# Output sums of a state-space layer moved behind head steps, keys in places of their own, the last state rows returned in two halves

## The chip, the cores and the metric

One Trainium2 chip, one of its cores. Times are microseconds of device time for one execution of the whole program. The engines are TensorE (PE; its weight loads are PEld), VectorE (DVE), ScalarE (ACT), GpSimd (POOL) and SyncE (SP), which here issues all the transfers.

## The reference: what is computed

One inference step of a two-layer decoder, 512 prompt tokens and 8 sample tokens (520 columns in all) of width 1024. Layer 0 mixes by a diagonal state-space model (S5: 48 groups of 16 channels, 64 states each) and by attention to 256 memory tokens; layer 1 attends to shared keys and values. The change lies in layer 0's mixing:

```python
y = (einsum('btgp,gcp->btgc', hr, c_re) - einsum('btgp,gcp->btgc', hi, c_im))
y = y.reshape(bsz, t, SEQ_WIDTH) + d_skip * u
y = gelu(y)
y = y * sigmoid(y @ w_glu + b_glu)            # w_glu is 768 x 768: six panels of 128 columns
...
s = einsum('bthd,bmhd->bhtm', q, mk) * ATTN_SCALE   # memory attention of the 8 sample rows
p = softmax(s)
```

All 16 results (both outputs, states, keys, values, convolution tails) are returned.

## The kernel before, in words

The state-space part runs in three thirds (`THIRDS`), t = 0, 1, 2, of 16 groups each. For a third, TensorE turns the input matrices (`bT` jobs, in `bp`), multiplies them with the inputs (`V` jobs), VectorE turns that by powers of the poles, scans it and writes the chunk states `hp`; TensorE makes the short kernels (`K` jobs), ScalarE copies them to `kern`, SyncE spreads `kern` by eight transfers into the block matrix `toep`. The output sums (`Y` jobs, `y_sums(t)`) need `hp` and `toep` of their third. ScalarE copies the sums to `yb`, SyncE writes them to a scratch area in DRAM (`y_store`, nine transfers that reorder rows) and reads them back in the layout of the residual (`y_return`, into `yz`); GpSimd adds them to the skip term (`add_z`), ScalarE applies the Gelu, and VectorE and ScalarE split the result into a high and a low part, `x_hi` and `x_lo`, for the gate's product. The gate's product (`glu`) is six panels, each 6 k-steps of 6 matmuls. Jobs of TensorE that go to the four `misc` banks take them in the order that `misc_jobs` lists; a job waits until the bank of the job four before it has been read.

Between these stand steps of the prompt's memory attention on TensorE (`head_step`, three steps in each of the last two thirds), and the memory attention of the 8 sample rows: a query product per row (`mem_query`), a product and a sum on VectorE (`mem_sample`), which needs the row's keys `mk`, then a softmax over all rows that goes back and forth: `decode_turn` (PE), `decode_spread` (DVE), `decode_max` (PE), `decode_shift` (DVE), `decode_exp` (ACT), `decode_sum` (DVE), `decode_total` (PE), `decode_scale` (DVE), then `mem_sums` (PE).

Every engine executes its own program strictly in the written order, and engines meet by semaphores only. In the order before, `y_sums(t - 1)` stands inside third t, between its `V` and its `K` jobs; `y_sums(2)` stands behind all head steps with two query products ahead of each half. Keys have six places, so that those of rows 6 and 7 are loaded behind the last state rows' return. VectorE does all eight `mem_sample` and the maximum before its first `x_lo`. In the lines of the profile L583 is the helper `load` on SyncE, L2706 the helper that turns a tile, L1206 VectorE's product helper, L2821 and L2826 the two kinds of matmul of `y_sums`, L2866 `mem_query`, L2555 `product`.

ScalarE's `hi(kb, q + 2)` rounds the weights for the panel after next; it reuses the place of panel q, and so waits for panel q to be done:

```python
if it is not None or q >= 2:
    act.wait_ge(panel_done, q - 1)
A.activation(w_hi[slot][:, 0:kb, :], raw[slot][:, 0:kb, :], ACT.Copy).then_inc(hi_made, 1)
```

## Time and profile before

| what | value |
|---|---|
| time before, median of 3 runs | 1567.71 us (1561.73 to 1569.77) |
| the profiled execution: its time | 1564.98 us |
| its span | 1562.6 us |
| busy, PE / PEld / DVE / ACT / POOL | 1425.3 / 1322.5 / 990.8 / 625.1 / 669.7 us |
| mean granted clock of TensorE | 0.957 of full speed (2.4 GHz) |

The span is what the trace covers; the profiled execution took 2.4 us more than its span. TensorE is busy for 91% of the span, but that share is a mean: the stretch of the change, from 160 to 282 us, is one where it stands still for a good part. The rows of the trace for that stretch are shown in a section below. In those, the time in brackets is how long the engine stood idle before the row, and what ended the idle time.

### The profile page before, as it was taken

How to read it: one execution, taken by the hardware profiler on the slowest of the kernel's cores; microseconds unless marked ns; L12 is line 12 of the kernel's file. 1: busy time of each engine (PE TensorE's matmuls, PEld its weight loads, DVE VectorE, ACT ScalarE, POOL GpSimd, SP SyncE). 2: the span in 40 equal slices, each digit the busy share in tenths (PEclk: the TensorE clock that was granted, in tenths of full speed). 3: DMA queues.
4: the chain of work that ended last, by engine and by line, in shares of the span. 5: the costliest groups of instructions: out<-in, count | busy, mean ns of one | idle time of the engine just before them, and what ended most of it. 6: DMA issues, size and time to landing. Idle time of an engine off the chain costs nothing.

```text
span 1562.6 us, 32532 instructions
## 1 busy us (share of the span) xinstructions
PE 1425.3 (91%) x12097; PEld 1322.5 (85%) x12097; DVE 990.8 (63%) x1649; ACT 625.1 (40%) x1058; POOL 669.7 (43%) x428
## 2 busy tenths in 40 slices
PE   6986858888998999999899989998989999999997
PEld 6975637878998999999798976556979999999997
DVE  5769945577776037775847688762677771367755
ACT  4554533345554123332415325541356651243323
POOL 0686332323433344443277888501314444344440
PEclk9996968989999999999999999999989999999999
DMA  5444372222333323232234859995212333233321
GB/s 171 125 98 77 63 195 73 76 62 56 88 90 91 89 81 93 82 101 80 60 114 129 237 157 291 331 349 158 81 50 81 94 102 86 81 94 89 107 80 60
DMA packets 288921, 180.46 MB, mean 115 GB/s; under 512 B 54088, under 2 KB 274412, under 8 KB 288764
## 3 DMA queue, kind: packets, MB, share of 16 engines
q1 hardware_dynamic: 288828, 179.20, 39.6%
q8 instruction: 61, 1.00, 0.3%
q14 instruction: 32, 0.26, 0.1%
HBM read 167.10 MB, written 10.63 MB: 114 GB/s over the span
## 4 chain that ended last, share of the span: by engine, by line
PE 62%; issue 13%; DVE 11%; POOL 5%; ACT 3%; SPq 2%; DMA 2%; DVEq 1%; ACTq 0%; POOLq 0%
PE big L2555 49%; PE big L2621 3%; PE misc L2706 2%; SPq L583 2%; ACT yc L2412 1%; DVE y L1667 1%; POOL s5s L926 1%; PE big L2904 1%; POOL e_tmp L926 1%; POOL e_r L926 1%; DVE tmp L1206 1%; POOL e_i L926 1%; PE misc L3103 1%; DVE rstd L1164 1%; PE big L2652 1%
## 5 line engine op out<-in xcount | busy, mean ns | idle before, releaser
L922 POOL TENSOR_TENSOR w_lo<-raw,w_hi 128x1024 fp32r<-128x1024 f32 (+2 forms) x162 | 425.2, 2626 | 722.8 <-ACT w_hi L2069 722.6
L2555 PE MATMUL big<-x_hi,w_hi 128*128 128x264 f32 x2008 | 415.0, 289 | 17.2 <-POOL w_lo L922 12.4
L2069 ACT ACTIVATE w_hi<-raw 128x1024 fp32r<-128x1024 f32 (+2 forms) x179 | 198.4, 1109 | 526.5 <-PE big L2555 490.6
L2555 PE MATMUL big<-x_hi,w_lo 128*128 128x264 f32 x2008 | 407.7, 285 | 0.0
L2555 PE MATMUL big<-x_lo,w_hi 128*128 128x264 f32 x2008 | 406.0, 284 | 0.0
L2555 PEld LDWEIGHTS big<-x_hi,w_hi 128*128 128x128 f32 x2008 | 312.2, 191 | 23.3 <-issue 16.3
L2555 PEld LDWEIGHTS big<-x_lo,w_hi 128*128 128x128 f32 x2008 | 311.7, 190 | 0.0
L2555 PEld LDWEIGHTS big<-x_hi,w_lo 128*128 128x128 f32 x2008 | 311.1, 190 | 0.0
L1756 DVE SCALAR_TENSOR_TENSOR yc<-uc,convw,yc 128x512 f32<-128x512 f32 x88 | 120.2, 1366 | 113.3 <-ACT yc L2412 113.3
L2555 PE MATMUL big<-h_hi,w_hi 128*128 128x264 f32 x616 | 126.1, 286 | 10.6 <-DVE h_lo L1771 9.1
L2555 PE MATMUL big<-h_lo,w_hi 128*128 128x264 f32 x616 | 124.8, 284 | 0.0
L2555 PE MATMUL big<-h_hi,w_lo 128*128 128x264 f32 x616 | 124.6, 284 | 0.0
L2555 PEld LDWEIGHTS big<-h_hi,w_hi 128*128 128x128 f32 x616 | 95.0, 190 | 11.8 <-DVE h_lo L1771 10.0
L2555 PEld LDWEIGHTS big<-h_lo,w_hi 128*128 128x128 f32 x616 | 95.3, 190 | 0.0
L2555 PEld LDWEIGHTS big<-h_hi,w_lo 128*128 128x128 f32 x616 | 95.3, 190 | 0.0
L1761 DVE SCALAR_TENSOR_TENSOR yc<-uc,convw,yc 128x512 f32<-128x512 f32 x88 | 84.7, 962 | 12.7 <-DVE yc L1759 0.2
L1784 DVE COPY y<-big 128x264 f32 (+1 forms) x32 | 12.2, 423 | 104.7 <-PE big L2555 104.7
L1059 POOL TENSOR_TENSOR areas<-areas,qb 128x768 f32<-128x768 f32 x41 | 74.6, 1833 | 8.7 <-DMA areas<-in_cache_k 7.9
L2412 ACT ACTIVATE yc<-uc,convw 128x520 f32<-128x520 f32 x88 | 72.3, 821 | 0.8
L1146 DVE TENSOR_TENSOR sumsq<-sumsq,sq 128x520 f32<-128x520 f32 x20 | 53.1, 2657 | 11.7 <-ACT sq L2368 9.9
L2408 ACT ACTIVATE newconv<-uc 128x10 f32 (+1 forms) x88 | 18.0, 205 | 103.9 <-DVE uc L1752 103.8
L2652 PE MATMUL big<-x_hi,w_hi 128*128 128x264 f32 (+1 forms) x96 | 38.2, 398 | 17.1 <-DVE x_lo L1196 16.5
(425 smaller groups left out, 2375.1 us busy)
## 6 DMA issues: line engine op xcount, KB each, us to landing
raw<-in_w_up SPq DMA_DIRECT2D x88, 512.0 KB, 3.9
raw<-in_w_down SPq DMA_DIRECT2D x32, 704.0 KB, 4.7
areas<-in_cache_v SPq DMA_DIRECT2D x42, 384.0 KB, 4.6
areas<-in_cache_k SPq DMA_DIRECT2D x41, 384.0 KB, 4.4
raw<-in_w_in SPq DMA_DIRECT2D x16, 512.0 KB, 4.2
raw<-in_w_out SPq DMA_DIRECT2D x16, 512.0 KB, 4.2
raw<-in_w_kv SPq DMA_DIRECT2D x12, 512.0 KB, 4.3
spare<-in_cache_k SPq DMA_DIRECT2D x12, 384.0 KB, 4.4
```

Of the source, the lines that this page charges most:

```text
L583: sp.dma_start(dst, src, **kw).then_inc(s_(sm), 16)
L922: pool.tensor_tensor(w_lo[slot][:, 0:kb, :], raw[slot][:, 0:kb, :], w_hi[slot][:, 0:kb, :].bitcast(F32), ALU.subtract).then_inc(lo_made, 1)
L926: own.do(pool.tensor_tensor(o, a_, b_, op))
L1059: own.tell(pool.tensor_tensor(p, p, qb[b % 2][:].rearrange("p (a d) -> p a d", a=2), ALU.mult), s_("k_product"), n + 1)
L1146: ins = V.tensor_tensor(sumsq[:], sumsq[:], sq[:, m % 2, :], ALU.add)
L1756: st(V.scalar_tensor_tensor(yy[:, 0:T], uu[:, 1:1 + T], w_[1], yy[:, 0:T], ALU.mult, ALU.add))
L1761: st(V.scalar_tensor_tensor(yy[:, 0:T], uu[:, 0:T], w_[0], yy[:, 0:T], ALU.mult, ALU.add))
L2069: A.activation(w_hi[slot][:, 0:kb, :], raw[slot][:, 0:kb, :], ACT.Copy).then_inc(hi_made, 1)
L2412: A.activation(yy[:], uu[:, 2:2 + NT], ACT.Identity, bias=convw[:, 1 - l, bass.ds(it + (f * KH + half * KF + 132), 1)], scale=convw[:, 1 - ...
L2555: ins = pe.matmul(big[2 * slot + b_][:, 0:c1 - c0], w[slot][:, k, :], r[:, c0:c1], start=(k == 0 and n_ == 0), stop=(k == kb - 1 and n_ == 2))
L2621: return pe.matmul(big[2 * slot + b_][:, 0:c1 - c0], w[slot][:, k, :], r[:, c0:c1], start=(k == 0 and n_ == 0), stop=(k == kb - 1 and n_ = ...
L2652: ins = pe.matmul(big[2 * slot + b_][:, 0:c1 - c0], w[slot][:, k, :], r[:, k, c0:c1], start=(k == 0 and n_ == 0), stop=(k == KD - 1 and n_ ...
```

## The change

Five edits, all in layer 0's state-space and gate part.

1. `y_sums(1)` moves from inside third 2 to the end of third 1, behind the head steps 3, 4 and 5. `y_sums(0)` stays. SyncE's `u_load(2)`, the states' return of thirds 0 and 1 and ScalarE's `read_y(1)` move with it.
2. The keys of the 8 sample rows have eight places of their own. Five are loaded inside third 2, ahead of `toep`'s last loading, one behind it, two behind the first gate weights.
3. The last third's output rows are stored in two halves of 8 groups, from a buffer of their own (`yb_last`), and returned in two tiles of 128 rows (`yz_last`); `add_z_tile`, the Gelu and the split follow tile by tile.
4. VectorE makes the `x_lo` of tiles 0 to 3 before `mem_sample` 4 and 5, then tiles 4 and 5, then `mem_sample` 6 and 7 and the maximum.
5. The softmax's steps move into the gate's six panels, each one panel or two later than before.

```diff
@@ y_sums in the list of jobs (and in the same way in TensorE's own code)
-        jobs += [("Y", t - 1, a) for a in range(TG // 4) if t]
+        jobs += [("Y", 0, a) for a in range(TG // 4) if t == 1]
         jobs += [("K", t, a) for a in range(TG // 4)] + [("qrow", 0, 1)] * (t == 0) + [("cT", t + 1)] * (t + 1 < THIRDS)
+        jobs += [("Y", 1, a) for a in range(TG // 4) if t == 1]
...
@@ SyncE
+            def y_return_tile(m):
+
+                if m == 0:
+                    sp.wait_ge(s_("y_out"), 16 * 9 * THIRDS)
+                else:
+                    sp.wait_ge(s_("y_rest_out"), 16 * 9)
+                load(yz_last[:, m, :], y_dram[(2 * THIRDS - 2 + m) * P:(2 * THIRDS - 1 + m) * P, :], "yz_rest_in" if m else "yz_in")
...
-                if t:
-                    full(sp, ("Y", t - 1, 3))
-                    if t + 1 < THIRDS:
-                        u_load(t + 1)
-                    y_store(t - 1)
+                if t == 1:
+                    full(sp, ("Y", 0, 3))
+                    y_store(0)
+                elif t == 2:
+                    y_return(0)
+                    full(sp, ("Y", 1, 3))
+                    y_store(1)
+                    full(sp, ("bT", 2, 3))
+                    for b in range(MK_EARLY + 1):
+                        mem_k(b)
+                    y_return(1)
                 sp.wait_ge(s_("s5_zero"), 2)
                 sp.wait_ge(s_("kern_ready"), 4 * (t + 1))
                 for tau in range(CHUNK):
                     load(toep[CH * tau:CH * tau + CH, :, (CHUNK - 1 - tau) * CH:P],
                          kern[:, :, 0:(tau + 1) * CH], "toep_in")
-                if t == THIRDS - 1:
-                    for b in range(MK_EARLY):
-                        mem_k(b)
-                if t:
-                    y_return(t - 1)
-
+                if t == 1:
+                    u_load(2)
+
+            mem_k(MK_EARLY + 1)
             sp.wait_ge(s_("hfin_made"), THIRDS)
             sp.wait_ge(s_("toep_in"), 16 * CHUNK * THIRDS)
             weights("glu", cols(I["w_glu"][0]), stop=2)
-            for b in range(MK_EARLY, MK):
+            for b in range(MK_EARLY + 2, NB):
                 mem_k(b)
             mem_v(0, mb[0])
-            y_store(THIRDS - 1)
-            y_return(THIRDS - 1)
+            y_store(THIRDS - 1, (0, TG // 2))
+            y_store(THIRDS - 1, (TG // 2, TG))
+            for m in range(2):
+                y_return_tile(m)
...
-            for b in range(MK, NB):
-                mem_k(b)
@@ VectorE
-            for b in range(4, NB):
-                mem_sample(0, mb[0], b)
-                if b in (5, 6):
-                    head_lo(0, FOX_PAIRS + b - 5)
-            mem_max(0, mb[0])
-
-            dve.wait_ge(s_("yz_used"), THIRDS)
+            for p in LAST[0]:
+                head_lo(0, p)
+
+            dve.wait_ge(s_("yz_used"), THIRDS - 1)
             for k in range(KS):
+                if k == KS - 2:
+                    mem_sample(0, mb[0], 4)
+                    mem_sample(0, mb[0], 5)
+                    dve.wait_ge(s_("yz_used"), THIRDS)
+                elif k == KS - 1:
+                    dve.wait_ge(s_("yz_used"), THIRDS + 1)
...
-                if k == 0:
-                    decode_spread(mb[0]["dst"], MEMH, ("mmaxT", 0), 1)
-            decode_shift(mb[0]["s"], MEMH, 2, ("mmax", 0))
-            decode_sum(mb[0]["s"], mb[0]["dst"], MEMH, 1)
+            for b in range(6, NB):
+                mem_sample(0, mb[0], b)
+            mem_max(0, mb[0])
             for m in range(KS):
                 gate_of(m)
                 if m == 0:
+                    decode_spread(mb[0]["dst"], MEMH, ("mmaxT", 0), 1)
+                elif m == 1:
+                    decode_shift(mb[0]["s"], MEMH, 2, ("mmax", 0))
+                elif m == 2:
+                    decode_sum(mb[0]["s"], mb[0]["dst"], MEMH, 1)
+                elif m == 3:
                     decode_scale(mb[0]["s"], mb[0]["dst"], MEMH, 2, ("mden", 0), 1)
@@ ScalarE
-            for t in range(THIRDS):
-                if t == THIRDS - 1:
-                    gelu(t)
-                glu_in(2 * t)
-                glu_in(2 * t + 1)
-            decode_exp(mb[0]["s"], 1)
+            for k in range(KS):
+                if k >= KS - 2:
+                    gelu(k)
+                    sync()
+                glu_in(k)
             for m in range(KS):
                 q = base + m
                 hi(kb if m + 2 < KS else KD, q + 2)
+                if m == 3:
+                    decode_exp(mb[0]["s"], 1)
                 act.wait_ge(panel_done, q + 1)
-                if m == 2:
+                if m == 0:
                     act.wait_ge(s_("mk_used"), NB)
@@ TensorE
-            y_sums(THIRDS - 1, two_queries)
+            two_queries(0)
+            y_sums(THIRDS - 1, lambda a_: two_queries(a_) if a_ else None)
...
-            decode_turn(("mmaxT", 0), dst, BM, 1)
...
-                if m == 0:
+                if m == 1:
+                    decode_turn(("mmaxT", 0), dst, BM, 1)
+                elif m == 2:
                     decode_max(("mmax", 0), dst, BM, 1)
-                elif m == 1:
+                elif m == 3:
                     decode_total(("mden", 0), dst, BM, 1)
-                elif m == 3:
+                elif m == 4:
                     mem_sums(0, mb[0])
```

How SyncE's queue stands before, from the first output sums' store on to the gate's first weights (the names are the destination and the source of each transfer; each `toep` loading is eight transfers, of which the first and the last are shown):

```order
L583 DMA u_87<-z_scratch 16x16x64 x8
...
L696 DMA y_scratch<-yb 16x16x64 x8
...
L583 DMA toep<-kern 16x2048
L583 DMA yz<-y_scratch 128x2x520
L696 DMA y_scratch<-yb 16x16x64 x8
...
L583 DMA toep<-kern 16x2048
L583 DMA mk_0_114<-in_cache_mem_k 128x2x256
...
L583 DMA yz<-y_scratch 128x2x520
L599 DMA raw<-in_w_glu 128x6x128 x2
```

And how it stands in the change:

```order
L703 DMA y_scratch<-yb 16x16x64 x8
...
L589 DMA toep<-kern 16x2048
L589 DMA u_87<-z_scratch 16x16x64 x8
...
L589 DMA yz<-y_scratch 128x2x520
L703 DMA y_scratch<-yb 16x16x64 x8
...
L589 DMA mk_0_116<-in_cache_mem_k 128x2x256
...
L589 DMA yz<-y_scratch 128x2x520
...
L589 DMA toep<-kern 16x2048
L589 DMA mk_5_121<-in_cache_mem_k 128x2x256
L605 DMA raw<-in_w_glu 128x6x128 x2
```

The inputs' load moved behind the second `toep` loading, and five keys' loads and the second return moved ahead of the third.

TensorE around the moved output sums, before (`bp` turns, `V` products of `u` and `bT`, the first output sums, and behind all sixteen groups of them the `K` products):

```order
L2706 MATMUL misc<-ident,bp 128x128 x16
L2978 MATMUL misc<-u_87,bT 64x72 x32
L2821 MATMUL misc<-hp_97,cp_99 64x72 x8
L2826 MATMUL misc<-u_96,toep 64x72 x4
...
L2995 MATMUL misc<-cp_67,bb_64 16x128 x32
```

And in the change:

```order
L2972 MATMUL big<-mem_tok,mprobT_106 64x64 x8
L2855 MATMUL misc<-hp_99,cp_101 64x72 x8
L2860 MATMUL misc<-u_98,toep 64x72 x4
...
L2740 MATMUL misc<-ident,bp 128x128 x16
L3012 MATMUL misc<-u_87,bT 64x72 x32
L3029 MATMUL misc<-cp_67,bb_64 16x128 x32
```

The output sums of third 1 now follow the last head step's product and stand ahead of the third 2's turns.

ScalarE at the start of the gate, before (`ms` are the scores in the exponential, `w_hi` the rounded weights of the panel after next):

```order
L2244 ACT_TABLE_LOAD
L2244 ACTIVATE ms_108<-ms_108 128x64
L2069 ACTIVATE w_hi<-raw 128x768
L2339 ACT_TABLE_LOAD
L2339 ACTIVATE gate<-big,gains 128x264
L2340 ACTIVATE gate<-big,gains 128x256
```

And in the change, at the gate's fourth panel:

```order
L2104 ACTIVATE w_hi<-raw 128x768
L2279 ACT_TABLE_LOAD
L2279 ACTIVATE ms_110<-ms_110 128x64
L2373 ACT_TABLE_LOAD
L2373 ACTIVATE gate<-big,gains 128x264
L2374 ACTIVATE gate<-big,gains 128x256
```

The exponential and its two table loads moved from before the first panel's rounding to behind the fourth's.

## Rows read from the trace of the kernel before

**Rows 1.** SyncE's issuing in order of time: start, duration, instruction, count.

```profile
162.49 5.95 SPq L583 DMA_DIRECT2D u<-z_scratch  x10
...
198.02 6.00 SPq L583 DMA_DIRECT2D toep<-kern  x8
204.06 3.49 SPq L583 DMA_DIRECT2D mk<-in_cache_mem_k  x4
...
212.08 0.95 SPq L583 DMA_DIRECT2D mv<-in_cache_mem_v  x1
222.20 4.18 SPq L696 DMA_DIRECT2D y_scratch<-yb  x8
...
228.86 0.38 SPq L583 DMA_DIRECT2D yz<-y_scratch  x1
...
231.87 0.92 SPq L583 DMA_DIRECT2D mk<-in_cache_mem_k  x2
```

**Rows 2.** TensorE in order of time, last third: start, duration, what, idle before.

```profile
178.82 3.67 PE L2706 MATMUL misc<-ident,bp 128*128 128x128 f32 x16 [3.05 <-DVEq L83]
183.27 2.22 PE L2978 MATMUL misc<-u,bT 128*64 128x72 f32 x64 [0.78 <-issue]
...
191.92 3.67 PE L2995 MATMUL misc<-cp,bb 64*16 64x128 f32 x64
...
208.11 2.05 PE L2866 MATMUL misc<-qrow,sel 128*128 128x256 f32 x4 [6.95 <-DMA toep<-kern]
210.09 0.76 PE L2821 MATMUL misc<-hp,cp 64*64 64x72 f32 x16
...
215.55 1.93 PE L2866 MATMUL misc<-qrow,sel 128*128 128x256 f32 x4
217.95 0.48 PE L2821 MATMUL misc<-hp,cp 64*64 64x72 f32 x16 [0.47 <-ACT yb L2116]
```

**Rows 3.** Second `toep` loading, its eight DMAs, from issue to landing.

```profile
DMA to landing us min/median/max: 1.9/3.3/3.9
```

**Rows 4.** Two `mk` loadings at 209 us, from issue to landing.

```profile
DMA to landing us min/median/max: 6.2/6.7/7.3
```

**Rows 5.** The `mv` loading (memory values), from issue to landing.

```profile
DMA to landing us min/median/max: 12.1/12.1/12.1
```

**Rows 6.** VectorE in order of time, around its scans and the last keys.

```profile
190.18 0.69 DVE L1206 TENSOR_TENSOR tmp<-e_r,v 128x512 f32<-128x512 f32 x1 [0.27 <-DVE cp L1299]
...
201.27 0.38 DVE L1580 COPY hp<-h 128x64 f32<-128x64 f32 x2
...
235.02 0.69 DVE L1347 TENSOR_TENSOR mprod<-mk,misc 128x512 f32<-128x512 f32 x1 [8.00 <-DMA mk<-in_cache_mem_k]
```

**Rows 7.** Windows of 1 us: busy by engine, granted clock (PEclk), DMA.

```profile
217.00:218.00 1.00, 0.53 (x6) 0.08 (x5) 0.97 (x2) 0.69 (x2) 0.70 (x3) 0.90 1.10 349
247.00:248.00 1.00, 1.00 (x6) 1.00 (x6) 0.48 (x2) 0.00 (x0) 0.00 (x0) 0.54 0.00 0
```

**Rows 8.** GpSimd and then ScalarE in order of time, last output sums.

```profile
232.76 2.37 POOL L1030 TENSOR_TENSOR y<-y,yz 128x1040 f32<-128x1040 f32 x1 [4.82 <-DMA yz<-y_scratch]
...
236.41 2.24 ACT L2110 ACTIVATE x_hi<-y 128x512 fp32r<-128x512 f32 x4
```

**Rows 9.** TensorE in order of time, around the gate's six panels.

```profile
241.95 0.77 PE L2555 MATMUL big<-x_hi,w_hi 128*128 128x264 f32 x2 [0.95 <-DVE x_lo L1632]
...
253.95 0.30 PE L2851 MATMUL misc<-mdst,ones 128*128 128x32 f32 x2
```

**Rows 10.** ScalarE and then VectorE in order of time, gate's panels.

```profile
238.66 1.28 ACT L2244 ACT_TABLE_LOAD   x1
249.97 0.26 ACT L2244 ACTIVATE ms<-ms 128x64 f32<-128x64 f32 x1 [10.03 <-DVEq L83]
...
258.75 0.85 ACT L2069 ACTIVATE w_hi<-raw 128x768 fp32r<-128x768 f32 x1 [2.97 <-PE big L2555]
...
260.36 2.10 DVE L1325 TENSOR_TENSOR gate<-gate,y 128x512 f32<-128x512 f32 x1 [2.36 <-ACT gate L2340]
```

More of the change, by code:

```diff
@@ L272, in page_in @@
     i = b - QB_PAGE
[L273 removed]
+    return (f"page_in{b}", 16 * page_use(n)) if i < 0 else (f"mkpage_in{i}", 16 * (page_use(n) + 2 * (i < NB // 2)))
 def page_before(n):
@@ L1048, in s5_beside @@
                     lo(base + i, (base + i) % 2, kb)
-                add_z(THIRDS - 1)
+                for m in range(2):
+                    add_z_tile(m)
             def k_products(first, stop):
@@ L2314, in _ @@
             copy_turned(0, 7)
-            gelu(1)
+            for k in range(KS - 2):
+                gelu(k)
+            sync()
             read_y(THIRDS - 1)
@@ L3007, in _ @@
                     head_step(0, n)
+                if t == 1:
+                    y_sums(1)
             pe.wait_ge(s_("qrow_ready"), 1)
```

67 lines of the change are left out of this document (37 added, 30 removed).

## The prediction

> **What bounds the kernel now.** I read the page first: TensorE is busy for 91% of the span, so a change can only give back time in which TensorE stands still. Then I read the windows of the stretch from 160 to 282 us, TensorE's rows in order of time, and last the rows of the engines that it waits for. In this stretch the end is set by one thread that passes from engine to engine. ScalarE has the last third's short kernels copied, SyncE spreads them into `toep` by eight transfers from 198.02 to 204.02 us [rows 1], the last lands near 208.1, and TensorE, idle for 6.95 us, goes on at 208.11 with four matmuls of query products for 2.05 us and only then with the output sums, at 210.09 [rows 2]. They have half clock until about 217.1, since the window from 217 to 218 shows 0.90 (nine tenths of it at 2.4 GHz, before it 1.2) [rows 7]. The first half of the sums takes 5.5 us, the next queries 1.93, and the second half, from 217.95 on [rows 2], some 3.3 at full clock: it ends at 221.2. A microsecond later SyncE stores the rows, reads them back from 228.86 on [rows 1], GpSimd adds them from 232.76 for 2.37 us, ScalarE applies the Gelu and from 236.41 splits the last two tiles [rows 8]. Beside this runs a second thread: the keys of rows 6 and 7 are loaded at 231.87 [rows 1], VectorE stands still for 8.00 us for them until 235.02 [rows 6], and its first `x_lo` comes behind them and the maximum. So the gate's first panel begins at 241.95, and the second is done by 253.95 [rows 9]. From there on the gate's panels follow each other.
>
> **The last third's sums start earlier.** The old place put the sums of third 1 (6.5 us from the end of the `V` products to the `K` products [rows 2]) into the thread of the last third. In the new place they wait for the second `toep`. The first sums are over at 162.4, just before SyncE's load of the inputs at 162.49 (5.95 us) [rows 1]; that load now comes last. The nine stores take 4.65 us (4.18 for eight [rows 1], 0.47 for the ninth), so with the copies' microsecond `toep` is issued from 168.1 to 174.1, and the last of its eight lands 3.9 us [rows 3] after its issue at 173.5: I put the start of the sums at 178.0 in place of 185.5. TensorE's head steps are over by then. Its clock is at half again here. How long it stays there I take from two other places: dense work began at 208.11 [rows 2] and the clock rose 9 us later, dense work began at 241.95 [rows 9] and the clock rose in the window from 247 to 248 (0.54) [rows 7], 6 us later. Sixteen groups cost 11 us at half clock and 6.5 at full, so with 6 us at half the sums take 9.0 and end at 187.0. Turns and `V` products follow; before they took from 178.82 to 185.49 [rows 2], at full clock I take 6.3, to 193.3. VectorE's scans, which began at 190.18 and ended at 201.65 [rows 6], thus begin at 193.9 and end at 205.3. The `K` products take 3.67 [rows 2] to 197.0, the copies 1.4: `kern` is ready at 198.4, against 198.0. So the sums taken out of the thread gain nothing by themselves, for the time is spent ahead of the turns. SyncE in the meantime stores third 1's rows from 188.0 to 192.7, issues five keys (four took 3.49 us, [rows 1], so 4.4) and one return, and is free at 197.6: hidden, by 0.8 us only. `toep` lands at 198.4 + 5.4 + 3.9 = 207.7. The scans (205.3) are hidden by 2.4 us.
>
> What is won is the order: the queries' 2.05 us are done beforehand, in time that TensorE spends waiting. The sums start at 207.7 in place of 210.09; first half to 213.2, queries to 215.1, second half with 2 us at half clock and 2.0 at full to 219.2. That is 2.0 us earlier than 221.2.
>
> **Two halves and two tiles.** From the end of the sums to the store is 1.0 us; the second half's nine transfers again take 4.65 us (half the bytes each, but the issue is what costs), so halving the rows adds nine issues, of which the first nine lie ahead of the end of the sums (from 214.2). From the start of the store to the return's issue it was 228.86 - 222.20 = 6.66 us [rows 1], from there to GpSimd's start 3.9 [rows 8]. For the second tile: 220.2 + 6.7 + 3.9 = 230.8. Its add is half of 2.37, its Gelu 0.6, its split of two rows 1.1 (2.24 for four [rows 8]), `x_lo` and signals 0.8: 234.5. The first tile comes some 2 us ahead of it. Four of six k-steps of panel 0 are done by then, since tiles 0 to 3 wait for nothing of the last third, and only one step of 1.3 us at half clock remains: panel 0 ends at 236. Before it started at 241.95 and took 7.2. The keys' thread is gone from this place: all keys are there by 220, and rows 4 to 7 cost VectorE 0.69 for each product and each sum [rows 6], rows 4 and 5 before tile 4 arrives, rows 6 and 7 behind tile 5, beside the panels.
>
> Panel 1 ran at full clock before. TensorE now stands still between the k-steps 3, 4 and 5, so I take panel 1 at 6 us of half clock again, 7.2 us in all, to 243.2. Against 253.95 [rows 9] that is 10.7 us gained.
>
> **What the softmax's new places cost.** In the new order `decode_total` stands behind panel 3 and needs `decode_sum`, and that the exponential. On ScalarE the exponential stands behind the rounding of panel 5's weights, which waits for panel 3 to be done. So it can start only when TensorE arrives where its result is wanted. The wait: signal 0.2, rounding 0.85, table load 1.28, exponential 0.26 [rows 10], sum and signals on VectorE 0.4, together 3.0 us of standstill. Before, the exponential's table was loaded at 238.66, while ScalarE was waiting [rows 10], and no panel waited. Behind it the sigmoid needs its table again (1.28), so gate 3 begins at 0.2 + 1.6 (258.75 to 260.36 [rows 10]) + 2.8 = 4.6 us after panel 3, takes 2.3 (2.10 and the sample columns), and the scaling 0.7: 7.6. TensorE is through panel 4 at 3.1 + 4.3 = 7.4, so `mem_sums` waits 0.3 more; its own time is the same in both orders. What follows panel 5 is as before: VectorE has no backlog by then. The other steps (turn behind panel 1, maximum behind panel 2) come 2 us and more ahead of use.
>
> **Sum.** 10.7 - 3.3 = 7.4 us. The profiled execution's own time is 1564.98 (span 1562.6): it would be 1557.6. It is 2.7 us below the median of the runs shown; from the median it would be 1560.3. I forecast between the two, **1559 us**.
>
> **One rule against it.** The memory values (2 MB, issued at 212.08 [rows 1]) are in flight when the first half of the rows is stored. Two keys issued into traffic took 7.3 us at most [rows 4]. Since the second half is stored only at 220.2, the sum above charges nothing for this. The Trainium skill ("DMA: Bandwidth & Descriptors", section "Queues, rings and completion order") says that each DMA engine consumes descriptors in the order of its ring, and that a completion signal lands only after that engine's earlier writes. By that rule the first half's stores complete no sooner than the values; the sum stays 1559 unless the values land behind the second half's stores too, which is the first rival below, 1563. No row of this trace shows that pair.
>
> **Rivals.**
> - *Queueing (0.22).* The values now go out later, for the gate's weights ahead of them wait for the final states, which follow the scans (3.7 us later). The values took 12.1 us from issue to landing [rows 5], so from 216 they would land at 228. If both halves of the rows wait for them, the second tile is returned at 228.5 in place of 226.9, and keys in front of `toep`, issued into traffic, take 1 to 2 us more than I gave. Gain 7.4 - 1.6 - 2 = 3.8: 1563. For it: two keys' loads took up to 7.3 [rows 4]; against: in the trace the rows' stores at 222.20 were issued while the values were landing, and cost nothing.
> - *The clock stays up (0.15).* TensorE has dense work from 207.7 on, then queries and k-steps. If the gaps behind k-step 3 are too short for the clock to fall, panel 1 takes 4.4 in place of 7.2 and the rest of panel 0 0.6 less; if it also rises early in the moved sums, 1.5 more. Gain 11 to 12: 1555. Against: before the panel at 241.95, too, TensorE had single query products between gaps, and it began at half clock [rows 7, 9].
> - *SyncE in front of `toep` (0.10, the side on which it is slower).* Five keys and a return now stand ahead of `toep`'s last loading. If each issue takes 1.9 us instead of 0.87 (four in 3.49 [rows 1]), SyncE is free at 202.6, 4.2 us late, and if `toep` then needs 7.3 [rows 4] in place of 3.9 [rows 3], the sums are 7.6 us late; with 9 us of half clock in the moved sums 1.3 more. 7.4 - 8.9: 1.5 slower, 1569. It decides from 7.4 us of lateness on, `toep` landing after 215.1.
> - *The moved work gives nothing back (0.05).* Panel 0's last k-step decides and comes no sooner; with the 3.3 us of standstill, 1571.
>
> The forecast's own cases (gain 4 to 11) hold 0.48.
>
> **Range and chances.** A measurement of this kernel tells a difference from none above some 0.5%, 7.8 us. My 7.4 lies right at it. Of the forecast's cases 0.27 and all 0.15 of the clock's count as faster, 0.42; its other 0.21, queueing and 0.04 of SyncE's case as the same, 0.47; slower are 0.06 of SyncE's case, where it comes together with what I have not seen, and the last one, 0.11. The range goes from 1551 (clock case, 4 us lower by the spread of the runs) to 1569.
>
> **What the profile after would show.** `y_sums(1)` starting at 178 and ending at 187; the third `toep` issued at 198.4; output sums at 207.7 with no queries ahead; gate's first panel with gaps before k-steps 4 and 5 and its end at 236; TensorE idle for 3 us behind the fourth panel and a table load of 1.28 right ahead of `decode_total`; `mem_sums` behind the fifth. It would be wrong if `toep` landed after 210, if the second tile came after 233, or if the exponential were found earlier.

## The result, and the profile after

| | median | runs |
|---|---|---|
| before | 1569.2 us | 7, from 1561.73 to 1572.67 |
| after | 1564.45 us | 7, from 1546.83 to 1575.57 |

The ratio of after to before is 0.9895 with an interval from 0.9848 to 0.9943; the medians differ by 4.75 us, 0.3%. (Every ratio here leaves out runs that are more than 1.5% above the fastest of their kernel, in after the three from 1573 to 1576 us; the experiments below show that these are no disturbance, so 0.9895 flatters the change.) The profiled execution of after took 1550.14 us, with a span of 1548.3 and a clock of 0.957, so it is 14.84 us shorter than the profiled one of before. The two traces were compared at a mark that both have: ScalarE's roundings of weights (`w_hi`), one for each of the 179 panels, numbered from 0.

| rounding | before | after | difference |
|---|---|---|---|
| 19, at the end of the gate's panel 1 | 254.21 | 243.88 | -10.33 |
| 21, panel 3 | 263.07 | 253.16 | -9.91 |
| 23, panel 5 | 273.80 | 268.80 | -5.00 |
| 24, the first behind the gate | 289.07 | 284.41 | -4.66 |
| 32, first feed-forward layer, up products | 361.91 | 357.37 | -4.54 |
| 56, behind these up products | 521.28 | 504.60 | -16.68 |
| 176, near the end | 1509.96 | 1495.60 | -14.36 |

So the difference has two main parts. Up to the end of the change's own stretch it is **4.66 us**; some 12 more come in the first feed-forward layer's up products, which no edit touches, and 2.3 are lost again after it. Of the 4.66, 1.47 were there before anything that the edit touches: the first output sums, whose place is the same in both kernels, begin that much earlier. TensorE before and then after:

```profile
155.88 0.48 PE L2821 MATMUL misc<-hp,cp 64*64 64x72 f32 x16
```

```profile
154.41 0.48 PE L2855 MATMUL misc<-hp,cp 64*64 64x72 f32 x16
```

Over all traces of this document they begin from 154.20 to 155.88 us with before's code and from 154.13 to 156.72 with after's, so this is a difference of executions. Counted from there, the edit's own gain in this pair of traces is 3.2 us; the mean over more traces is below. First the own stretch. SyncE's issuing in the profile after, in order of time, which answers to [rows 1]:

```profile
167.01 5.20 SPq L589 DMA_DIRECT2D toep<-kern  x8
...
192.75 3.58 SPq L589 DMA_DIRECT2D mk<-in_cache_mem_k  x5
196.42 0.41 SPq L589 DMA_DIRECT2D yz<-y_scratch  x1
198.33 5.81 SPq L589 DMA_DIRECT2D toep<-kern  x8
...
214.46 5.60 SPq L703 DMA_DIRECT2D y_scratch<-yb_last  x8
...
220.57 3.78 SPq L703 DMA_DIRECT2D y_scratch<-yb_last  x8
...
225.25 2.36 SPq L589 DMA_DIRECT2D yz_last<-y_scratch  x2
```

The last line holds two issues, one at 225.25 and one at 227.26. TensorE in order of time, for [rows 2] and [rows 9] (rows with idle time, then the window of the moved sums: its length, the busy time of PE, PEld, DVE, ACT and POOL, the granted clock, the DMA engines' share and GB/s; the clock of 0.50 is 1.2 GHz):

```profile
208.03 0.76 PE L2855 MATMUL misc<-hp,cp 64*64 64x72 f32 x16 [5.90 <-DMA toep<-kern]
...
226.91 0.77 PE L2589 MATMUL big<-x_hi,w_hi 128*128 128x264 f32 x2 [3.94 <-DVE x_lo L1662]
...
236.01 0.50 PE L2589 MATMUL big<-x_hi,w_hi 128*128 128x264 f32 x2 [2.91 <-DVE x_lo L1662]
...
255.97 0.41 PE L2885 MATMUL misc<-mdst,ones 128*128 128x32 f32 x2 [2.90 <-DVEq L83]
```

```profile
180.00:184.00 4.00, 4.00 (x76) 3.20 (x72) 3.90 (x4) 0.82 (x2) 0.49 (x1) 0.50 0.52 140
```

GpSimd's two tiles and VectorE's low parts, for [rows 8] and [rows 6]:

```profile
227.98 1.93 POOL L1056 TENSOR_TENSOR y<-y,yz_last 128x520 f32<-128x520 f32 x1 [2.17 <-DMA yz_last<-y_scratch]
230.09 1.95 POOL L1056 TENSOR_TENSOR y<-y,yz_last 128x520 f32<-128x520 f32 x1 [0.18 <-DMA yz_last<-y_scratch]
```

```profile
224.06 8.00 DVE L1662 TENSOR_TENSOR x_lo<-y,x_hi 128x512 fp32r<-128x512 f32 x8 [1.84 <-ACT x_hi L2145]
231.99 0.67 DVE L1374 TENSOR_TENSOR mprod<-mk,misc 128x512 f32<-128x512 f32 x1
...
234.85 2.16 DVE L1662 TENSOR_TENSOR x_lo<-y,x_hi 128x512 fp32r<-128x512 f32 x4
```

The output sums begin at 208.03 and end at 219.2, `x_lo` is complete at 237.0, panel 0 ends at 238.5, panel 1 at 243.6. The 8.00 us that VectorE waited for keys [rows 6] are gone. Behind panel 3 TensorE stands still for 2.90 us. ScalarE shows why ([rows 10] for before), and the window behind it what followed:

```profile
253.16 0.84 ACT L2104 ACTIVATE w_hi<-raw 128x768 fp32r<-128x768 f32 x1 [3.27 <-PE big L2589]
254.02 1.28 ACT L2279 ACT_TABLE_LOAD   x1
255.31 0.26 ACT L2279 ACTIVATE ms<-ms 128x64 f32<-128x64 f32 x1
255.59 1.28 ACT L2373 ACT_TABLE_LOAD   x1
```

```profile
257.00:261.00 4.00, 4.00 (x23) 4.00 (x22) 1.73 (x4) 0.73 (x2) 0.00 (x0) 0.57 0.49 135
```

The clock was at 1.2 GHz from 257.3 to 260.7 us (0.57 in this window), in the panel behind the standstill, which took 5.9 us instead of the 4.3 of a panel at full clock.

The other part. In the trace of before the roundings of the up products come in pairs, 3.0 and 9.3 us apart in turn; in that of after each comes 5.77 us after the last. ScalarE, GpSimd, VectorE and TensorE in before, one round of 12.3 us, in order of time for each engine:

```profile
399.09 1.06 ACT L2069 ACTIVATE w_hi<-raw 128x1024 fp32r<-128x1024 f32 x1
...
402.13 1.06 ACT L2069 ACTIVATE w_hi<-raw 128x1024 fp32r<-128x1024 f32 x1 [0.16 <-PE big L2555]
407.15 0.21 ACT L2408 ACTIVATE newconv<-uc 128x10 f32 x1 [3.97 <-DVE uc L1752]
...
411.41 1.06 ACT L2069 ACTIVATE w_hi<-raw 128x1024 fp32r<-128x1024 f32 x1
```

```profile
400.23 2.38 POOL L922 TENSOR_TENSOR w_lo<-raw,w_hi 128x1024 fp32r<-128x1024 f32 x1 [6.89 <-ACT w_hi L2069]
403.26 2.39 POOL L922 TENSOR_TENSOR w_lo<-raw,w_hi 128x1024 fp32r<-128x1024 f32 x1 [0.64 <-ACT w_hi L2069]
```

```profile
397.01 0.75 DVE L1761 SCALAR_TENSOR_TENSOR yc<-uc,convw,yc 128x512 f32<-128x512 f32 x1
...
403.45 2.75 DVE L1761 SCALAR_TENSOR_TENSOR yc<-uc,convw,yc 128x512 f32<-128x512 f32 x1
...
406.26 0.42 DVE L1751 TENSOR_TENSOR uc<-big,rstd 128x264 f32<-128x264 f32 x1
```

```profile
402.75 0.50 PE L2555 MATMUL big<-x_hi,w_hi 128*128 128x264 f32 x2 [0.66 <-POOL w_lo L922]
...
415.06 0.50 PE L2555 MATMUL big<-x_hi,w_hi 128*128 128x264 f32 x2 [0.51 <-POOL w_lo L922]
```

The rows form a circle (`w_lo` is the low part of a panel's weights, which GpSimd subtracts out behind each rounding; `yc` is a convolution on VectorE). Two roundings close together bring two `w_lo` close together. VectorE's convolution step, 0.75 us alone, takes 2.75 beside the second. So VectorE takes over the next panel only at 406.26, ScalarE gets it at 407.15, has work of its own for 4.3 us, and comes to the next rounding at 411.41, late although its panel was long done (no idle time before it), close to the one behind it. TensorE waits for `w_lo` once in each round. (The Trainium skill, "SBUF — State Buffer", section "Who interferes with whom", says that a VectorE instruction with two inputs in SBUF contends with a GpSimd instruction that reads SBUF; this one has two, and it ends 0.55 us behind the `w_lo` that began before it.) In after the same engines stand like this, ScalarE, then VectorE, then GpSimd:

```profile
392.59 1.06 ACT L2104 ACTIVATE w_hi<-raw 128x1024 fp32r<-128x1024 f32 x1 [0.61 <-PE big L2589]
...
398.35 1.06 ACT L2104 ACTIVATE w_hi<-raw 128x1024 fp32r<-128x1024 f32 x1 [2.19 <-PE big L2589]
...
404.12 1.06 ACT L2104 ACTIVATE w_hi<-raw 128x1024 fp32r<-128x1024 f32 x1 [0.61 <-PE big L2589]
```

```profile
388.86 2.06 DVE L1791 SCALAR_TENSOR_TENSOR yc<-uc,convw,yc 128x512 f32<-128x512 f32 x1 [1.28 <-ACT yc L2446]
...
396.30 0.80 DVE L1791 SCALAR_TENSOR_TENSOR yc<-uc,convw,yc 128x512 f32<-128x512 f32 x1 [1.33 <-ACT yc L2446]
```

```profile
387.96 2.42 POOL L939 TENSOR_TENSOR w_lo<-raw,w_hi 128x1024 fp32r<-128x1024 f32 x1 [2.93 <-ACT w_hi L2104]
```

Here, too, one convolution step in two panels is slowed beside a `w_lo` (2.06 us), but no rounding is late for it. Every rounding waits for TensorE: TensorE is the bound, and two panels take 11.53 us. The pairs also cost at the end of the stage: in before TensorE waits 4.42 us at 502.17 for the last `h_lo`, and the clock is low from 500.5 to 507.3; in after that wait is 1.57 us and the clock stays up. From rounding 32 to 56 it is 159.37 us in before, 147.23 in after. That the slowed step holds the pairs together is read from these rows; no run took it away.

What broke the pairs in after? In both traces TensorE waits ahead of the third up panel for `w_lo`, 3.36 us in before (to 365.52) and 3.37 in after (to 360.98). Windows of 4 us behind it, before and then after:

```profile
366.00:370.00 4.00, 4.00 (x36) 4.00 (x35) 3.77 (x5) 0.00 (x0) 2.19 (x1) 1.00 0.54 147
```

```profile
362.00:366.00 4.00, 4.00 (x21) 4.00 (x20) 3.21 (x5) 0.50 (x2) 1.62 (x1) 0.50 0.63 186
```

In before the clock stayed up, in after it was low from 359.7 to 366.5 us. The panels took longer, rounding 35 came 5.53 us behind 34 rather than 3.03, and the circle didn't close. This was my theory when the experiments began: a low clock of 6.8 us made the run shorter by 12.

### The profile page after: what moved, and what is told of

Its sections match the earlier page's. It is cut to its first block, busy times and chain, and to the rows that moved or that the text cites. A ratio compares the mean times of both kernels' runs of the same rounds, so it can differ in the third digit from the quotient of the medians.

```text
span 1548.3 us, 32542 instructions
## 1 busy us (share of the span) xinstructions
PE 1429.6 (92%) x12097; PEld 1327.1 (86%) x12097; DVE 984.6 (64%) x1649; ACT 623.2 (40%) x1057; POOL 674.5 (44%) x429
## 4 chain that ended last, share of the span: by engine, by line
PE 73%; issue 12%; DVE 8%; SPq 2%; ACT 2%; DMA 2%; POOL 1%; DVEq 0%; ACTq 0%; POOLq 0%
PE big L2589 59%; PE big L2655 3%; PE misc L2740 2%; SPq L589 1%; PE misc L2855 1%; ACT w_hi L2104 1%; PE misc L2860 1%; POOL w_lo L939 1%; DVE tmp L1233 1%; PE big L2938 1%; DVE y L1702 1%; PE big L2686 1%; DMA toep<-kern 1%; DVE x_lo L1662 1%; PE misc L3141 1%
## 5 line engine op out<-in xcount | busy, mean ns | idle before, releaser
L2104 ACT ACTIVATE w_hi<-raw 128x1024 fp32r<-128x1024 f32 (+2 forms) x179 | 198.4, 1109 | 561.9 <-PE big L2589 526.5
L1791 DVE SCALAR_TENSOR_TENSOR yc<-uc,convw,yc 128x512 f32<-128x512 f32 x88 | 133.7, 1519 | 113.3 <-ACT yc L2446 113.3
L1796 DVE SCALAR_TENSOR_TENSOR yc<-uc,convw,yc 128x512 f32<-128x512 f32 x88 | 66.1, 752 | 12.7 <-DVE yc L1794 0.2
L1173 DVE TENSOR_TENSOR sumsq<-sumsq,sq 128x520 f32<-128x520 f32 x20 | 53.2, 2658 | 11.7 <-ACT sq L2402 9.9
L2145 ACT ACTIVATE x_hi<-x,gains 128x264 fp32r<-128x264 f32 (+2 forms) x64 | 35.4, 561 | 35.6 <-DVE x L1708 28.0
```

The source lines that it names most:

```text
L1173: ins = V.tensor_tensor(sumsq[:], sumsq[:], sq[:, m % 2, :], ALU.add)
L1791: st(V.scalar_tensor_tensor(yy[:, 0:T], uu[:, 1:1 + T], w_[1], yy[:, 0:T], ALU.mult, ALU.add))
L1796: st(V.scalar_tensor_tensor(yy[:, 0:T], uu[:, 0:T], w_[0], yy[:, 0:T], ALU.mult, ALU.add))
L2145: ins = A.activation(o, src, ACT.Copy, scale=1.0 if g is None else g)
```

## The experiments

Twelve kernels, four under each of the three headings below; those under one heading ran on one chip, beside 7 to 25 runs of the kernel before.

### Both kernels again, a delay, a fill

**before_again** and **after_again** are the two kernels as they are.

> The kernel before, unchanged, for a second profile on another chip. My theory of the result: the edit itself gives 4.7 us (the first weight rounding behind the gate began at 289.07 before and at 284.41 after); the other 10 us of the difference between the two profiled runs come from the up products of the first feed-forward layer, which no edit touches. There the trace of before has weight roundings in pairs (12.3 us for two panels), that of after has them evenly (11.5 us for two). If this is a state that each run falls into or not, this profile may show either; in pairs I expect a span near 1562, evenly one near 1552. The rival, that the edit itself brings the even order, expects pairs and a span near 1562 here every time.

Measured: median 1567.84 us (10 runs, 1553.67 to 1579.77), ratio to before 0.9986 (0.9946 to 1.0026). The profiled run, 1566.91, has pairs in the first layer's up products and none in the second's.

> The changed kernel, unchanged, for a second profile. My theory: the first rounding behind the gate again near 284.4 us; the up products evenly or in pairs, with a span near 1548 or 1558 accordingly, and a ratio to before of 0.997 (4.7 us) if both are in the same order. The rival, that the edit itself brings the even order, expects it evenly and a ratio near 0.99.

Measured: median 1556.35 us (10 runs), ratio 0.9948 (0.9910 to 0.9987). The profiled run, 1551.37, is even in both layers, and rounding 24 came at 285.72. Its runs form two groups, five from 1546.85 to 1552.06 and five from 1560.64 to 1564.48. The 25 runs of before beside them: four from 1555.43 to 1559.09, twenty from 1563.58 to 1573.68, one of 1579.43. The groups are 11 to 12 us apart in both kernels: the price of one stage in pairs.

The rival, that the edit itself brings the even order, isn't wholly beaten. The edit doesn't force that order, but it seems to go with it more often: of all 74 runs of the kernel before, 9 lie in the lowest group (below 1560 us); of the 17 of the changed kernel, 8 do (below 1556). If the runs are independent draws, so large a difference would come up by chance in about 3 of 1000 cases. The groups are told by their times, not by traces, and how the edit would shift the odds stays open.

**before_delay** is before with one late panel, in the first layer alone:

```diff
...
+ product(up + 2, (up + 2) % 2, KD, xs_, HALF)
+ pe.wait_ge(lo_made, up + 4)
+ pe.wait_ge(panel_read, up + 2)
+ for _ in range(22):
+     pe.matmul(big[2 * ((up + 3) % 2)][:, 0:256], x_hi[:, 0, 0:P], x_hi[:, 0, 0:256], start=True, stop=True)
+ product(up + 3, (up + 3) % 2, KD, xs_, HALF)
```

> The kernel before, with 22 matmuls of no use (some 2.6 us at full clock, written to a bank that the panel then overwrites) ahead of the fourth panel of the first up products, and the third and fourth panel taken out of the loop. My theory: one panel that ends late is enough to space the roundings evenly, as in the trace of after; the delay costs 2.6 us once, and the stage gives back some 12: 9 to 10 us less than before, with the roundings 5.8 us apart. The rival, that the even order comes from the edit at the state-space tail (its clock or its transfers), expects the pairs back within a few panels and 2.6 us more than before.

Measured: median 1556.29 us (10 runs, nine of them from 1553.85 to 1559.05), ratio 0.9929 (0.9899 to 0.9959). The profiled run had intervals of 7.1 and then 5.8 us. Work of no use, put into the kernel before, made it 11.5 us shorter; the theory had 9 to 10, the rival 2.6 longer. (In the profiled run the clock was also low from 363.8 to 367.2, ahead of the delay; before_spaced, below, is even in this stage with no low clock.) It differs from before in these lines alone, so the even order needs no edit at the state-space tail.

**after_fill** puts such matmuls into TensorE's wait ahead of the third panel of the first layer:

```diff
...
+ pe.wait_ge(panel_read, up + 1)
+ for _ in range(27):
+     pe.matmul(big[2 * (up % 2)][:, 0:256], x_hi[:, 0, 0:P], x_hi[:, 0, 0:256], start=True, stop=True)
```

> The changed kernel, with 27 matmuls of no use (some 3.2 us) in the time in which TensorE waits ahead of the third panel of the first up products, so that its clock has no reason to fall there; the third and fourth panel are taken out of the loop. My theory: the late panel that set the roundings apart was late because the clock was low from 359.7 to 366.5 us; without that the pairs of before return, and the run takes some 12 us more than the run of after that was profiled (1562). The rival, that the clock has nothing to do with it, expects the time of the changed kernel, 1550, with the roundings 5.8 us apart.

Measured: median 1554.41 us (4 runs), ratio 0.9898 (0.9823 to 0.9974). This missed: the stage was even, with the clock up throughout. The matmuls had begun 1.4 us behind the wait's start and so ended at 358.8, 1.5 us after `w_lo` was ready: the fill was itself a delay. But the second layer of this run, where nothing was filled in, had no low clock there and had pairs (from rounding 120 to 144 it took 172.16 us, in after_again 160.01). after_short_fill, below, mends the experiment.

### The exponential, the halves, and the fill again

**exp_early**:

```diff
+ if m == 3:
+     decode_exp(mb[0]["s"], 1)
  hi(kb if m + 2 < KS else KD, q + 2)
- if m == 3:
-     decode_exp(mb[0]["s"], 1)
```

> The changed kernel, with ScalarE's exponential of the memory softmax ahead of the rounding of panel 5's weights instead of behind it. My theory: the exponential then runs while TensorE works on panel 3, so the 2.90 us in which TensorE stood still behind that panel are gone, and with them the low clock from 257.3 to 260.7 us that followed, 1.5 us: panel 5 ends 4 us earlier than in a run of the changed kernel, counted from the end of panel 2. The rival, that the sigmoid's table has to be loaded twice in any order and only moves the wait to the gate's read-out of panel 3, expects the 2.9 us to turn up behind panel 4 or at the memory sums, and no gain.

Measured: median 1553.36 us (10 runs), ratio 0.9877 (0.9840 to 0.9914; the medians of all runs stand at 0.9905). ScalarE and then TensorE in its profile:

```profile
251.03 1.28 ACT L2279 ACT_TABLE_LOAD   x1
...
254.28 0.85 ACT L2104 ACTIVATE w_hi<-raw 128x768 fp32r<-128x768 f32 x1 [1.70 <-PE big L2589]
255.15 1.28 ACT L2373 ACT_TABLE_LOAD   x1
```

```profile
254.02 0.30 PE L2885 MATMUL misc<-mdst,ones 128*128 128x32 f32 x2
```

The total has no idle time before it, and the second table load is there as before but is covered by panel 4. From rounding 20 to 23 it took 16.42 us instead of after's 20.49: 4.07 less, as expected. No low clock followed. In two traces with the standstill, after_fill and one_store, none followed either, so the move wins the 2.9 us in every run and the 1.5 of the clock in most.

**one_store** stores the last rows whole (`y_store(THIRDS - 1)`), and returns them as two tiles.

> The changed kernel, with the last third's rows stored in one piece by nine transfers behind the end of the sums, as before the change, and still returned as two tiles. My theory: in the trace of after both tiles are returned together at 225.25 us, behind the second half's nine stores, so the halves gain nothing and the gate's panels end where they did (within 0.5 us). The rival, my prediction's sum, has the first tile 2 us ahead of the second because of the halves, and expects the first panel's end to be later by up to 2 us without them.

Measured: median 1562.25 us (10 runs), ratio 0.9979 (0.9938 to 1.0019), with pairs in the first layer of the profiled run. From the end of the output sums to the second tile's return it took 7.5 us, in the nine traces with two halves 7.7 to 8.5; to rounding 21 it took 33.0, in those 33.1 to 34.1 (xlo_first, below, apart). The halves gain nothing, as the theory said, but not for its reason. In after the two tiles weren't returned together: each return waited for the ninth store of its own half, landed at 225.23 (5.1 us after its issue) and at 227.25, so the first was issued 2.0 us ahead. In one_store the returns were issued at 228.25 and 228.64, and yet GpSimd's adds began 2.0 us apart here too, since the first add took 1.85:

```profile
231.06 1.85 POOL L1053 TENSOR_TENSOR y<-y,yz_last 128x520 f32<-128x520 f32 x1 [3.29 <-DMA yz_last<-y_scratch]
```

**after_spaced** and **after_short_fill** put 27 and 13 of the matmuls shown above ahead of the third panel in both layers.

> The changed kernel, with 27 matmuls of no use ahead of the third panel of the first up products of both layers (3.3 us from 355.3 us on in the run with them in the first layer alone, of which 1.5 us reached beyond the wait). My theory: a panel that ends at least 1.5 us late spaces the roundings evenly, so no run has pairs in either layer: the spread of the runs goes from 18 us to under 8, the median is that of the fast runs of the changed kernel, 1548 to 1552. The rival, that pairs and even spacing are drawn anew whatever stands ahead, expects two groups of runs 12 us apart as with the changed kernel.

> The same with 13 matmuls instead of 27 in each layer, 1.6 us: they end before the weights for the third panel are ready (the wait is 3.4 us), and so delay nothing, but leave TensorE only some 0.3 us without work there. My theory: the clock then doesn't fall in the third and fourth panel, no panel is late, and the roundings pair up in both layers: 12 us in each over the even order, a time of 1570 to 1575. The rival, that the low clock from 359.7 us on was not what spaced the roundings in the trace of after, expects the times of the changed kernel, 1547 to 1564, with either order by chance.

Measured: after_spaced 1546.66 us (4 runs, 1545.44 to 1551.12), ratio 0.9859 (0.9809 to 0.9910); after_short_fill 1575.42 (10 runs, all from 1572.07 to 1577.60), ratio 1.0050 (1.0029 to 1.0072). TensorE and then ScalarE in after_short_fill, where the matmuls end ahead of `w_lo`:

```profile
361.18 1.81 PE L3093 MATMUL big<-x_hi 128*128 128x256 f32 x13 [1.42 <-DVE uc L1787]
363.17 0.50 PE L2589 MATMUL big<-x_hi,w_hi 128*128 128x264 f32 x2 [0.18 <-POOL w_lo L939]
```

```profile
371.98 1.06 ACT L2104 ACTIVATE w_hi<-raw 128x1024 fp32r<-128x1024 f32 x1
375.00 1.06 ACT L2104 ACTIVATE w_hi<-raw 128x1024 fp32r<-128x1024 f32 x1 [0.16 <-PE big L2589]
```

And the same in after_spaced, where they reach 1.5 us beyond it:

```profile
355.26 3.50 PE L3093 MATMUL big<-x_hi 128*128 128x256 f32 x27 [1.42 <-DVE uc L1787]
```

```profile
366.07 1.06 ACT L2104 ACTIVATE w_hi<-raw 128x1024 fp32r<-128x1024 f32 x1
370.32 1.06 ACT L2104 ACTIVATE w_hi<-raw 128x1024 fp32r<-128x1024 f32 x1 [1.38 <-PE big L2589]
```

The clock is up in both. With 13 matmuls the third interval is 3.02 us and both layers are in pairs, with 27 it is 4.25 and both are even. The medians are 28.8 us apart; between the two traces the stages account for 13.6 and 13.1. So the order can be set either way by how late one panel is. It also explains the three runs of after from 1573 to 1576 us: their times are those of two layers in pairs, though no trace of them was seen.

The other traces fit. The fourteen traces hold 28 such stages (the first half of each layer's up products), 12 of them with the delay or the 27 matmuls, all even. Of the 16 others nine had a low clock within 10 us behind the third panel's rounding, and all nine were even; seven had none (two of them those of after_short_fill), and all seven were in pairs. In the second layer of before and before_again the clock was low for 3.4 us only; the third interval was 4.6 us, and that was enough.

### What the edit itself brings, and the rest of its parts

All four kernels of this part carry the 27 matmuls in both layers, so that the up products are even; `before_spaced` is the kernel before with them.

> The kernel before, with the 27 matmuls of no use ahead of the third panel of the first up products of both layers, so that its roundings there are evenly spaced in every run, as those of the changed kernel with the same matmuls (1546.7 us). The difference of the two is then what the edit itself brings. My theory, from the first rounding behind the gate in the traces so far (289.1 and 289.3 before; 284.4, 285.7 and 281.1 after): 5 us, so 1551 to 1553. The prediction's sum says 7.4, so 1554. The rival, that the whole measured difference is the edit's, expects 1560 or more.

Measured: 1555.98 us (4 runs, 1554.00 to 1558.24), ratio 0.9891 (0.9837 to 0.9945); after_spaced had 0.9859 on another chip. The ratios differ by 0.0032, 5 us, but their intervals overlap; the medians differ by 9.3, on two chips (the kernel before took 1568.29 on the one and 1571.46 on the other). 1555.98 lies between the theory's 1551 to 1553 and the rival's 1560. More exact is rounding 24: 289.07, 289.30, 288.89 and 287.99 in the four traces with before's code up to there; 284.41, 285.72, 281.05, 280.62 and 286.54 in the five with after's. The means are 288.81 and 283.67: **5.1 us**, but from 1.5 to 8.7 for one trace against another. Counted from the start of the first output sums, which no edit touches, the means are 133.66 and 128.73: 4.9 us, and from 2.1 to 8.2.

**sums_back** moves `y_sums(1)`, ScalarE's `read_y(1)` and the return back to the last third.

> The changed kernel with the 27 matmuls, and with third 1's output sums back in the thread of the last third (between the value products and the kernel products, with their stores ahead of the last spreading of the short kernels and their return behind it). The prediction's step says that the sums taken out of the thread gain nothing, for the same time is spent ahead of the turns: then this run ends the last sums within 1 us of the changed kernel, and takes 1547. A rival: ahead of the turns the sums ran wholly at half clock (11.0 us from 176.54 to 187.5 in the trace of after, against 6.5 at full clock), so the move lost up to 2 us, and this run is faster, 1545. The other: they hid behind the second spreading after all, and this run is 3 to 5 us slower, 1550 to 1552.

Measured: 1551.80 us (4 runs), ratio 0.9870 (0.9814 to 0.9927). SyncE, then TensorE:

```profile
199.37 2.50 SPq L588 DMA_DIRECT2D mk<-in_cache_mem_k  x5
201.97 6.08 SPq L588 DMA_DIRECT2D toep<-kern  x8
```

```profile
211.89 0.76 PE L2854 MATMUL misc<-hp,cp 64*64 64x72 f32 x16 [9.00 <-DMA toep<-kern]
```

`kern` is ready at 199.0, against 199.5 to 199.9 in the two kernels of this chip with the sums in front: as predicted, the sums taken out of the thread gain nothing there. But SyncE now comes to `toep` 3.0 us behind `kern`, because the rows' stores and five keys stand ahead, and the sums end at 222.1 instead of 220.4 and 220.7. With the five keys where the change puts them, the move is worth 1.5 us, because it takes SyncE off the path, not TensorE. Neither rival's cause held; the second one's sign did, and the median lies in its range, on a chip where no run of the unaltered change stands beside it.

**xlo_first** moves VectorE's rows 4 and 5 behind the low parts.

> The changed kernel with the 27 matmuls, and with VectorE's rows 4 and 5 of the memory scores behind the low parts of all six tiles, with rows 6 and 7. In the trace of after VectorE made these rows from 231.99 to 234.85 us while the last two tiles' Gelu and high parts were done by 234.0, and their low parts followed only at 234.85 to 237.0. My theory: panel 0 ends 1 to 2 us earlier, of which panels 1 to 3 keep it all: 1545 to 1546. The rival, that the rows then press on the maximum and the softmax behind panel 3, expects the same time as the changed kernel or up to 1 us more.

Measured: 1551.40 us (4 runs), ratio 0.9863 (0.9810 to 0.9916). `x_lo` was complete at 236.8, 1.5 us earlier than in the next kernel (238.3), but:

```profile
242.49 1.28 ACT L2371 ACT_TABLE_LOAD   x1 [3.74 <-DVE ms L1377]
```

ScalarE's read-out of panel 0 waits for all eight rows' keys (`mk_used`), since the gate lies in their place, and stood still for 3.74 us. Rounding 21 came at 255.79, against 254.50 in the next kernel. The theory fell. The rival had up to 1 us more; it was 1.3 at this mark, by a wait that neither had named.

**best** is exp_early with the 27 matmuls.

> The changed kernel with the exponential ahead of the rounding of panel 5's weights and the 27 matmuls of no use in both layers: the two remedies together. My theory: they are independent, so the median is that of the changed kernel with the matmuls, 1546.7, less 4 us (5.0 us were won between the fourth panel's rounding and the first one behind the gate in the profile of the early exponential, of which a low clock that also falls away without it in some runs made 1.5): 1542 to 1543, with a spread below 8 us. The rival: the earlier gate moves the clock's falls and something later gives the gain back, 1545 to 1547.

Measured: 1544.29 us (4 runs, 1541.31 to 1544.87), ratio 0.9813 (0.9760 to 0.9866): 11.7 us below before_spaced and 27.2 below before (1571.46) on the same chip, the lowest median of all here, between the theory's 1542 to 1543 and the rival's 1545 to 1547. From rounding 21 to 24 it took 27.52 us, against after_spaced's 31.39 and 30.87 and 30.88 in the other two traces of the changed kernel on this chip: 3.4 to 3.9 gained, 4 expected.

What the early keys and the tile-wise adding bring by themselves wasn't tried apart. That they hold the bulk of the 10.3 us is argued from the rows: the wait of 8.00 us for keys is gone, the halves gain nothing, the moved sums 1.5. The queries taken ahead weren't tried apart either; the row at 208.03 shows the sums beginning as soon as `toep` lands.

## Why the prediction was right, and where it wasn't

The measured median, 1564.45 us, lies inside the range of 1551 to 1569 around the forecast of 1559. That it does is in good part luck: five of the seven runs of after lie outside that range, because each of two stages in pairs adds some 12 us, and no term of the prediction has that. What it can be held to is the edit's own gain, 7.4 us predicted.

| step | predicted | profile after |
|---|---|---|
| moved sums | 178.0 to 187.0 | 176.5 to 187.5 |
| scans | 193.9 to 205.3 | 193.9 to 205.4 |
| `toep` issued, output sums begin | 198.4, 207.7 | 198.3, 208.0 |
| output sums end | 219.2 | 219.2 |
| second tile at GpSimd | 230.8 | 230.1 |
| `x_lo` complete, panel 0 ends | 234.5, 236 | 237.0, 238.5 |
| panel 1 | 7.2 us, to 243.2 | 5.1 us, to 243.6 |
| standstill behind panel 3 | 3.0 us | 2.90 us |
| gain to the first rounding behind the gate | 7.4 us | 4.66 us |

- **The last third's sums start earlier: right**, and from the end of the moved sums on each step within 0.5 us. Two misses cancel in that. The whole trace was 1.5 us ahead of before's, and so the moved sums began at 176.5, as the last `toep` landed; but they had half clock all the time, not for 6 us, and took 11.0 us instead of 9.0. In after_spaced the clock rose at 178.7 and they took 7.6 us; its output sums ended at 216.1. That is the rival of the clock, in one trace of nine.
- **Two halves and two tiles: the sum right, its terms not.** "The first tile comes some 2 us ahead" was right, and gained nothing: in one_store GpSimd took the tiles 2 us apart without the halves, and rounding 21 was no later. An add took 1.95 us, not half of 2.37. "`x_lo` and signals 0.8" was mis-sized: VectorE needed 8.00 us for eight low parts beside GpSimd's work (1.0 each, against 0.54 in the last four), then two rows of scores, and the last low part came 5.0 us after the second tile's add ended. Panel 1 was given 7.2 us of half clock and took 5.1, with the clock up from 240.2 on, nearer to the clock rival's 4.4. The errors nearly cancel: 10.7 predicted, 10.33 measured, or 8.9 without the 1.47 us by which the whole trace was ahead.
- **What the softmax's new places cost: the mechanism right, the sum too small.** The 2.90 us, the table load and the rounding ahead of it are as predicted, and exp_early removed the standstill. Missing was what a standstill does to the clock behind it: 1.5 us in panel 4, in six of the eight traces that have the standstill. From rounding 21 to 23 it took 15.64 us against 10.73: 4.9 lost, 3.3 predicted. `mem_sums` waited for nothing, where 0.3 was charged (the prediction's own figures, 7.6 and 7.4, give 0.2). The turn and maximum between the panels cost another 0.4, given as nothing, and 0.3 went behind panel 5.
- **The sum** was 7.4; over all traces the edit brought 4.9 to 5.1. In the profiled pair it was 4.66, 2.7 less than predicted: 0.4 up to panel 1, 1.6 on the standstill with the clock behind it and `mem_sums`, 0.4 and 0.3 on the two terms given as nothing. The term that was missing is the clock behind the standstill.
- **The rule on queues** held no price, and none was paid on the second half: from its first store to its return it was 6.7 us, as before. The first half's stores landed 4.5 to 7.4 us after their issue, from 221.8 on, while the values (11.5 us from 211.44) landed at 222.9. "No sooner than the values" was not so for five of the nine stores. The rule of the Trainium skill that the prediction quotes is told of each DMA engine by itself; the prediction carried it over to whole transfers, which it doesn't order. The queueing rival's premise didn't come either: the values were issued at 211.44, not at 216, because the gate's weights went out only 1.2 us later than before (209.33) and the two keys behind them took 1.06 us to issue, not 2.83.
- **SyncE in front of `toep`** didn't come: SyncE was free at 196.8, 1.5 us ahead of `kern`. sums_back shows how near it was.
- **"A measurement tells a difference above 7.8 us"** took the spread for noise. It is an order of work in two stages of the feed-forward layers, each worth 12 us, and the prediction had no case for it. Whoever compared the ends of the two traces alone would have put all 14.8 us down to the change.

## What to carry to other kernels

Compare two traces at marks along the whole program, not at the end, and take one mark ahead of the first edit: here two thirds of the difference lay in code that no edit touched, and 1.5 us stood there before the change began. Where run times form groups, look for a loop of two panels whose intervals alternate; the rows here suggest that a helper engine slowed by its neighbour holds such an order for the whole stage, and the runs show that one late panel at the start can end it. An instruction that needs another function's table belongs ahead of the one that waits for TensorE, not behind it, and a standstill of 3 us should be priced with the clock that it may cost.

## What was not expected of the hardware

- A low clock of 6.8 us went with a run that was 12 us shorter, and 22 matmuls of no use made the kernel before 11.5 us shorter.
- A wait of 3.4 to 3.7 us ahead of the third up panel came with a low clock in some stages and in others not. The Trainium skill ("TensorE: Matmul & The Clock Gate", section "Part 1: The HAM clock gate") says that where the clock moves depends on a phase that varies from run to run; the traces agree, with nine of the fourteen stages that have this wait low and five not.
- VectorE's product with two inputs in SBUF took 2.75 us instead of 0.75 beside GpSimd's subtraction, and 2.06 in the even order.
